# Final normalisation moved into the expert loop, one pair late, with fewer gathered-row buffers and interleaved rows

## The chip, the cores and the metric

One NeuronCore of a Trainium2 chip runs the whole program. The metric is the device time of one execution in microseconds, lower is better. Engine names are those of the profile: PE is TensorE, DVE is VectorE, ACT is ScalarE, POOL is GpSimd, SP is SyncE, which here only issues DMAs.

## What is computed

One step of a one-layer decoder for 512 prompt and 64 sample tokens of width D = 1024, all in float32. Two mixer branches (sliding-window attention and gated linear attention) and a first layer norm come before the part that is changed: a mixture of 32 experts, of which each token takes two of one group of eight, followed by the last layer norm.

```python
combine = jnp.sum(one_hot(e_glob, 32) * w[..., None], axis=1)   # two experts per token, of one group
for e in range(N_EXPERTS):
    he = jax.nn.silu(t @ w_g[e]) * (t @ w_u[e])                  # 1024 -> 256, twice
    y = y + combine[:, e:e + 1] * (he @ w_d[e])                  # 256 -> 1024
hp = layer_norm(DN_ALPHA * hp + y, ln2_g[l], ln2_b[l])           # (x - mean) * rsqrt(var + eps) * g + b
```

## The kernel before

The program runs straight through: mixer branches until about 640 us, then a router, then the **expert loop** from about 667 to 919 us, then a last stage. Only the router's tables, the loop and the last stage are touched.

**Pairs.** The experts are worked in pairs: pair g holds experts 2g and 2g+1, and a tile of 128 rows has 64 places for the tokens of each. With these inputs there are 16 pairs: pairs 0 to 14 are written out (`FIXED` = 15) and pair 15 is the one turn of a counted loop, which takes an expert with more than 64 tokens too. One pair's weights are six DMAs of 1 MB (gate, up and down of two experts), issued by SP into three slots (`NSLOT`); SP waits, before it loads pair g+3, until PE has used pair g (`gu_full`, `dn_full`).

**Rows.** The router builds tables: column g of `tbi` holds for each of the 128 places of pair g the token's row in `h1_rows` (the first layer norm's output) and the row of `expert_rows` to which the result goes; `tbw` holds the weight. An empty place has a row past the end, which the DMA's bounds check leaves out. `expert_rows` has 2 x 576 rows, one for each token and choice. POOL issues the row DMAs: `gather` (L698) brings rows into one of four buffers `Xg` (`NX` = 4), `send` (L707) takes the result tile `Yt` to `expert_rows`. The first four gathers go ahead of the loop; then pair by pair `send(g)`, `gather(g+4)`.

**One pair, engine by engine.** PE in turn g: `gate_up(g+1)` (L2030), `turn_a(g)` (L2038, a transpose of the activations), `turn_x(g+2)` (L2017, a transpose of gathered rows), `down(g)` (L2052). ACT: `silu(g+1)` (L1034), `drain_at(g)` (L1038, a copy out of PSUM that `down(g)` needs), `drain_xt(g+2)` (L1024, and L1027, which scales the gathered rows for the residual). DVE: `gate(g+1)` (L1590), `drain_xt(g+2)` (L1584), `scaled(g)` (L1598 and L1600), which adds weighted expert rows to the scaled rows, half a tile each, and releases POOL's `send(g)` and PE's `down(g+1)` (`y_rows`). Each engine runs its own queue in the order written here.

**Last stage.** When POOL has seen the last `send` land (`loop_done`), SP reads both results of each token back in five tiles (`y0`, `y1`); DVE adds them (L1626), subtracts the mean, and after ACT's squares and root (L1056 to L1062) scales (L1637); SP stores each tile.

Of the kernel before, what the change touches and what calls it, by code (L numbers as in the profile page):

```python
# [19 lines left out]
P = 128  # L20
D = 1024
# [5 lines left out]
TILES = 5  # L27
# [13 lines left out]
MAX_PAIRS = 25  # L41
# [3 lines left out]
NX, NY = 4, 1  # L45
# [11 lines left out]
for _n, _w in (("ident", 128), ("tri", 128), ("ones", 128), ("scan", T), ("bias", 2048), ("sbias", 272),  # L57
               ("cmask", 64), ("smask", 64), ("bmask", 8), ("i4", 4), ("i8", 8), ("i4v", 20), ("inval", 10), ("restart", 160), ("vals", 20), ("pid", 1), ("plow", 1), ("eid", 32), ("e31", 32), ("evens", 9),
               ("iota", 128)):
    CONST[_n] = (_at, _w)  # L60
    _at += _w
# [94 lines left out]
def layout():  # L156
# [59 lines left out]
def decoder_kernel(nc, A, O):  # L216
# [15 lines left out]
    with ctx:  # L232
# [80 lines left out]
        tbi = ctx.enter_context(nc.sbuf_tensor("tbi", [P, 2, COLS], i32))  # L313
        tbw = ctx.enter_context(nc.sbuf_tensor("tbw", [P, COLS], f32))
        w2 = ctx.enter_context(nc.sbuf_tensor("w2", [RANK, GH * HK], f32))
        y0, y1, junk2 = sb("y0", [P, TILES, D]), sb("y1", [P, TILES, D]), sb("junk2", [P, D])
        lst = ctx.enter_context(nc.sbuf_tensor("lst", [1, 132], i32))
        idx = ctx.enter_context(nc.sbuf_tensor("idx", [P, 2, 2], i32))
# [13 lines left out]
        for n, w in (("lg", 5 * 36), ("gmax", 5), ("gt", 20), ("gmin", 5), ("goh", 20), ("eg", 20), ("gsum", 5),  # L332
# [3 lines left out]
                     ("hot", 10 * COLS), ("eg1", 1), ("t9", 9), ("n9", 1)):  # L336
# [11 lines left out]
        y_d = nc.dram_tensor("expert_rows", [2 * TQ, D], f32, kind="Internal").ap()  # L348
# [4 lines left out]
        y_sum = sem("y_sum")  # L353
        y_sq = sem("y_sq")
# [36 lines left out]
        rows_moved = sem("rows_moved")  # L391
        max_ready = sem("max_ready")
# [114 lines left out]

        def wait_y_free(eng, g):
# [17 lines left out]
        def _(sp):  # L526
# [34 lines left out]
            def expert(g, a):  # L561
                return slice(2 * g + a, 2 * g + a + 1)
# [46 lines left out]

            sp.wait_ge(loop_done, 1)  # L610
            for i in range(TILES):
                r = ROWS[i]
                sp.dma_start(y0[0:r, i, :], y_d[i * P:i * P + r, :]).then_inc(y_back[i], 16)
                sp.dma_start(y1[0:r, i, :], y_d[TQ + i * P:TQ + i * P + r, :]).then_inc(y_back[i], 16)
            for i in range(TILES):
                sp.wait_ge(y_ready, i + 1)
                dst = O[0][0, i * P:i * P + P, :] if i < 4 else O[1].rearrange("b t d -> (b t) d")
                sp.dma_start(dst, y0[0:ROWS[i], i, :]).then_inc(y_out, 16)
            sp.wait_ge(y_out, 16 * TILES)

        @block.gpsimd
        def _(pool):
# [13 lines left out]
            for b in range(2):  # L636
# [3 lines left out]
                OUTS[0] += 1  # L640

# [45 lines left out]
            pool.wait_ge(h1_stored, 16 * TILES)  # L687
            pool.wait_ge(tb_ready, 1)
# [13 lines left out]
            def send(g, rows):  # L702
# [6 lines left out]
                                        bounds_check=2 * TQ - 1, oob_is_err=False).then_inc(y_sent[n], 16)  # L709
# [3 lines left out]
            for g in range(FIXED):  # L713
                send(g, tbi[:, 1, g:g + 1])
                if g + NX <= FIXED:
                    gather(g + NX, tbi[:, 0, g + NX:g + NX + 1])
            pairs = pool.value_load(lst[0:1, 128:129], min_val=FIXED + 1, max_val=MAX_PAIRS)
            with pool.Fori(FIXED, pairs) as g:
# [3 lines left out]
                hold(g)  # L722
                pool.tensor_copy(idx[:, :, :], tbi[:, :, bass.ds(g, 2)]).then_inc(idx_ready, 1)
# [4 lines left out]
                n, k = y_place(g)  # L728
                pool.wait_ge(y_sent[n], k * 16 + 16)
                hold(g)  # L730
            pool.sem_inc(loop_done, 1)
# [7 lines left out]
        def _(act):  # L739
# [299 lines left out]

            drain_xt(0)  # L1040
            silu(0)
            drain_xt(1)
            for g in range(FIXED):
# [3 lines left out]
                if g + 2 <= FIXED:  # L1047
                    drain_xt(g + 2)
            act.wait_ge(list_ready, 1)
            pairs = act.value_load(lst[0:1, 128:129], min_val=FIXED + 1, max_val=MAX_PAIRS)  # L1050
            with act.Fori(FIXED, pairs) as g:
                silu(g)
                drain_at(g)
                drain_xt(g + 1)

            link(act.activation(epsc[:, 1:2], epsc[:, 0:1], ACT.Sqrt))  # L1056
            for i in range(TILES):
                r = ROWS[i]
                act.wait_ge(y_sum, i + 1)
                link(act.activation(junk2[0:r, :], y0[0:r, i, :], ACT.Square, bias=mv[0:r, i, 0:1],  # L1060
                                    accum_out=mv[0:r, i, 1:2]))
                act.activation(rstd[0:r, i:i + 1], mv[0:r, i, 1:2], ACT.Sqrt, scale=1.0 / D, bias=epsc[0:r, 0:1])\  # L1062
                   .then_inc(y_sq, 1)


        @block.vector
        def _(dve):
# [343 lines left out]
            dve.tensor_copy(R["val"][:, 0:20], cst("vals"))  # L1411
# [107 lines left out]
            link(dve.scalar_tensor_tensor(R["nt"], R["nt"], 64.0, cst("e31"), ALU.mult, ALU.add))  # L1519
# [657 lines left out]
```

## Time and profile before

| | us |
|---|---|
| median of three runs (lowest to highest) | 955.76 (953.86 to 956.06) |
| the profiled execution | 955.62 |
| its span in the trace | 952.9 |
| PE busy | 826.7 (87%) |
| DVE busy | 407.4 (43%) |
| ACT busy | 274.8 (29%) |
| POOL busy | 73.8 (8%) |

The mean granted TensorE clock is 0.923 of full speed. The chain that ended last is PE for 68% of the span, DMA for 12%, DVE for 9%, SP's queue for 7%. These are averages over stages that differ: the mixers are PE's, while the expert loop moves over 100 MB of weights. What a change in the expert loop does is read from that loop's own rows: which wait ends last before each piece of PE's work.

### The profile page before, as it was taken

To read this page: it belongs to the slowest core of one execution; us is meant where nothing else is said; L and a number is where in the kernel's file an instruction comes from. 1 tells how busy PE (TensorE), PEld (TensorE's weight loads), DVE (VectorE), ACT (ScalarE), POOL (GpSimd) and SP (SyncE) were. 2 spreads that over 40 slices of the span, in tenths; PEclk is the share of its full clock that TensorE was granted. 3 is DMA by queue.
4 is the path that set the end of the run, shared out by engine and by line. 5 is a ranking of instruction groups with operands and counts; after the bars stand their busy time and mean duration, and the time that the engine had idled before them with its cause. 6 is when DMAs were issued, how large, how long until landed. Compare 5 with 4: busy or idle time off the path is not lost.

```text
span 952.9 us, 12647 instructions
## 1 busy us (share of the span) xinstructions
PE 826.7 (87%) x5254; PEld 636.2 (67%) x5254; DVE 407.4 (43%) x785; ACT 274.8 (29%) x530; POOL 73.8 (8%) x96
## 2 busy tenths in 40 slices
PE   2799999998999999999999989984999697786850
PEld 1789999885788878899999988774433232332320
DVE  4456644569625555732314166556122111111118
ACT  6367112335324345522122242120211011011113
POOL 1200300000000000000000010001011100101010
PEclk8899999999699999999999999995899998899875
DMA  9221533101114342222222064167999999999726
GB/s 322 95 90 60 188 122 94 45 13 33 45 50 125 109 133 72 86 70 89 67 89 79 33 251 161 41 239 315 397 417 418 421 417 418 421 419 420 303 94 238
DMA packets 65367, 178.70 MB, mean 188 GB/s; under 512 B 7168, under 2 KB 41184, under 8 KB 52880
## 3 DMA queue, kind: packets, MB, share of 16 engines
q1 hardware_dynamic: 53792, 144.45, 40.3%
q0 software_dynamic: 10832, 31.04, 9.3%
q10 hardware_dynamic: 688, 2.43, 0.7%
q8 instruction: 41, 0.67, 0.3%
q14 instruction: 14, 0.11, 0.0%
HBM read 165.33 MB, written 21.36 MB: 196 GB/s over the span
## 4 chain that ended last, share of the span: by engine, by line
PE 68%; DMA 12%; DVE 9%; SPq 7%; ACT 3%; issue 1%; ACTq 0%; POOLq 0%; DVEq 0%
PE bank L1658 16%; PE bank L1660 15%; PE bank L1659 15%; DMA wgu<-in_w_exp_up 10%; PE bank L2030 7%; SPq L554 6%; PE bank L2052 2%; PE bank L1866 1%; SPq L558 1%; PE bank L1766 1%; DVE ring L1121 1%; PE bank L1886 1%; PE bank L1895 1%; PE bank L1962 1%; PE bank L1879 1%
## 5 line engine op out<-in xcount | busy, mean ns | idle before, releaser
L1658 PE MATMUL bank<-hT,ring 128*128 128x288 f32 (+2 forms) x608 | 184.0, 303 | 15.5 <-DVE ring L1121 13.5
L1660 PE MATMUL bank<-hT,ring 128*128 128x288 f32 (+2 forms) x608 | 181.4, 298 | 0.0
L2030 PE MATMUL bank<-wgu,XT 128*64 128x512 f32 x512 | 131.0, 670 | 39.5 <-DMA wgu<-in_w_exp_up 37.8
L1658 PEld LDWEIGHTS bank<-hT,ring 128*128 128x128 f32 (+1 forms) x608 | 114.8, 189 | 21.8 <-DVE ring L1121 14.2
L2030 PEld LDWEIGHTS bank<-wgu,XT 128*64 128x64 f32 x512 | 44.4, 154 | 124.2 <-issue 117.6
L1660 PEld LDWEIGHTS bank<-hT,ring 128*128 128x128 f32 (+1 forms) x608 | 114.6, 189 | 0.6
L1121 DVE TENSOR_TENSOR ring<-ring,ring 128x2048 fp32r<-128x2048 f32 (+2 forms) x32 | 68.0, 2126 | 96.7 <-ACT ring L787 96.6
L787 ACT ACTIVATE ring<-ring 128x2048 fp32r<-128x2048 f32 (+2 forms) x32 | 56.1, 1752 | 112.9 <-PE bank L1660 112.2
L1590 DVE TENSOR_TENSOR act<-bank,sil 128x256 f32<-128x256 f32 x16 | 6.8, 424 | 159.4 <-PE bank L2038 143.3
L1659 PE MATMUL bank<-hlo_r,ring 128*128 128x288 f32 x240 | 70.7, 295 | 0.0
L1659 PE MATMUL bank<-osb,ring 128*128 128x288 f32 (+2 forms) x224 | 68.2, 304 | 0.0
L1034 ACT ACTIVATE sil<-bank 128x256 f32<-128x256 f32 x16 | 6.2, 385 | 195.8 <-PE bank L2030 195.8
L2052 PE MATMUL bank<-wd,aT 128*64 128x512 f32 x256 | 58.5, 598 | 1.2 <-ACT aT L1038 1.2
L1658 PE MATMUL bank<-ring,hT 128*128 128x256 f32 (+3 forms) x200 | 57.4, 288 | 0.4 <-ACT hlo_ln L938 0.4
L1659 PE MATMUL bank<-ring,hT 128*128 128x256 f32 (+3 forms) x200 | 56.0, 281 | 0.0
L1659 PEld LDWEIGHTS bank<-hlo_r,ring 128*128 128x128 f32 x240 | 45.2, 188 | 0.0
L1660 PE MATMUL bank<-ring,osb 128*128 128x256 f32 (+3 forms) x160 | 44.1, 277 | 0.0
L1659 PEld LDWEIGHTS bank<-osb,ring 128*128 128x128 f32 (+1 forms) x224 | 42.7, 190 | 0.6
L1659 PE MATMUL bank<-hlo_ln,ring 128*128 128x288 f32 x144 | 42.6, 296 | 0.0
L1658 PEld LDWEIGHTS bank<-ring,hT 128*128 128x128 f32 (+1 forms) x200 | 36.8, 184 | 4.9 <-issue 3.3
L1660 PE MATMUL bank<-gv,ring 128*128 128x288 f32 x128 | 37.7, 295 | 0.0
L1659 PE MATMUL bank<-gq,ring 128*128 128x288 f32 x128 | 37.7, 294 | 0.0
(351 smaller groups left out, 1485.6 us busy)
## 6 DMA issues: line engine op xcount, KB each, us to landing
wgu<-in_w_exp_gate SPq DMA_DIRECT2D x32, 1024.0 KB, 22.9
wgu<-in_w_exp_up SPq DMA_DIRECT2D x32, 1024.0 KB, 25.1
wd<-in_w_exp_down SPq DMA_DIRECT2D x32, 1024.0 KB, 27.0
ring<-in_w_in SPq DMA_DIRECT2D x17, 1024.0 KB, 5.2
ring<-in_w_in SPq DMA_DIRECT2D x8, 512.0 KB, 4.6
s<-in_state_gla POOLq DMA_DIRECT2D x4, 1024.0 KB, 6.1
out<-s POOLq DMA_DIRECT2D x4, 1024.0 KB, 5.1
ring<-in_w_gla_br SPq DMA_DIRECT2D x4, 1024.0 KB, 5.3
```

Of the source, the lines that this page charges most:

```text
L554: sp.dma_start(wgu[n][a][:, half], A[w][0][e, :, :].rearrange("e (p k) f -> p (e k) f", p=P))\
L558: sp.dma_start(wd[n][a][:, :, :], A["w_exp_down"][0][e, :, :].rearrange("e (p k) n -> p (e k) n", p=P))\
L787: act.activation(dst, src, ACT.Copy).then_inc(w_hi, 1)
L1121: dve.tensor_tensor(dst, src, high, ALU.subtract).then_inc(w_split, 1)
L1658: pe.matmul(out, sh, mh, start=first, stop=False)
L1659: pe.matmul(out, sh, ml, start=False, stop=False)
L1660: return pe.matmul(out, sl, mh, start=False, stop=last)
L1766: ins = pe.matmul(bk[:, c:c + 256], q, kT[rows, (a - 1) * P:(a + 1) * P], start=True, stop=True)
L1866: ins = pe.matmul(bk[:, 0:HV], kem[r:r + 64, b, c // 2, :], gv[r:r + 64, c // 2, gcol], start=True, stop=True)
L1879: pe.matmul(bk[:, 0:HV], am[:, b, i * P:i * P + P], gv[:, i, gcol], start=True, stop=False)
L2030: ins = pe.matmul(bk[t, :].rearrange("p (h f) -> p h f", h=2), XT[:, kc, t], wgu[n][a][:, :, kc, :], start=(kc == 0), stop=(kc == KC - 1))
L2052: ins = pe.matmul(psum[5 + half][t, :], aT[:, kc, t], wd[n][a][:, kc, 512 * half:512 * half + 512], start=(kc == 0), stop=(kc == 1))
```

## The change

1. **Last stage into the loop.** `expert_rows` becomes `first_rows` with one row per token. Experts are paired as g and g+16, so the two experts of a token (one group of eight) are never in one pair. The result of a token's first expert goes to `first_rows`; when its second expert's pair comes, those rows are fetched from there (`previous`) into one of two buffers `Pv`, added to that pair's `Yt`, normalised, and stored straight to the outputs. `tbi` gets two more columns for each pair: the rows to fetch (the same numbers serve the store to the prompt output), and the rows of the sample output.
2. **One pair late.** In turn g DVE runs `added(g-1)` ahead of `scaled(g)` and `normal(g-1)` behind it; ACT runs `squares(g-1)` behind `drain_xt(g+2)`, with a table load for the root and one back to Silu; POOL runs `finish(g-1)`, two stores, and `previous(g+1)`, behind `send(g)` and `gather(g+3)`. What is left of pair 14 stands between the written-out turns and the counted loop.
3. **Buffers.** `NX` goes from 4 to 3. `first_rows` is set once from the inputs, early, by two DMAs of POOL's queue, and both `Pv` buffers are zeroed.
4. **Interleaved rows.** Place k of an expert's 64 is no longer partition k of its half: eight neighbouring places stand four partitions apart.
5. **Tables.** `COLS` goes from 26 to 34; a pair past the sixteenth now holds 128 rows of one expert (none with these inputs).

```diff
-MAX_PAIRS = 25
+MAX_PAIRS = 33
 COLS = MAX_PAIRS + 1
-NX, NY = 4, 1
+NX, NY, NP = 3, 1, 2
@@ SP
             def expert(g, a):
-                return slice(2 * g + a, 2 * g + a + 1)
+                return slice(g + 16 * a, g + 16 * a + 1)
-            sp.wait_ge(loop_done, 1)
-            for i in range(TILES):
...
-            sp.wait_ge(y_out, 16 * TILES)
+            sp.wait_ge(rows_out, pairs * 32)
+            sp.sem_inc(all_stored, 1)
@@ POOL
+            pool.dma_start(y_d[0:SEQ, :], A["x_prompt"][0]).then_inc(y_set, 16)
+            pool.dma_start(y_d[SEQ:TQ, :], A["x_sample"].rearrange("b t d -> (b t) d")).then_inc(y_set, 16)
...
+            def previous(g, rows):
+                n, k = y_place(g - 1) if isinstance(g, int) else (FIXED % NY, g + (FIXED // NY - FIXED - 1))
+                pool.wait_ge(y_sent[n], k * 16 + 16)
+                hold(g)
+                n, k = prev_place(g)
+                pool.indirect_dma_start(out=Pv[n], out_offset=None, in_=y_d[:, :],
...
+            def finish(g, prompt, sample):
+                if not isinstance(g, int) or g:
+                    pool.wait_ge(z_ready, g)
+                    hold(g)
+                    rows = Ut
...
+                pool.indirect_dma_start(out=O[0][0], out_offset=bass.IndirectOffsetOnAxis(ap=prompt, axis=0), in_=rows,
+                                        in_offset=None, bounds_check=SEQ - 1, oob_is_err=False).then_inc(rows_out, 16)
+                pool.indirect_dma_start(out=O[1].rearrange("b t d -> (b t) d"),
...
                 if g + NX <= FIXED:
                     gather(g + NX, tbi[:, 0, g + NX:g + NX + 1])
+                if g == 0:
+                    pool.wait_ge(finish_ready, 1)
+                if g:
+                    finish(g - 1, tbi[:, 2, g - 1:g], tbi[:, 3, g - 1:g])
+                previous(g + 1, tbi[:, 2, g + 1:g + 2])
+            finish(FIXED - 1, tbi[:, 2, FIXED - 1:FIXED], tbi[:, 3, FIXED - 1:FIXED])
@@ ACT
+            def squares(g):
+                step(act.activation(epsc[:, 1:2], epsc[:, 0:1], ACT.Sqrt), g, 1)
+                act.wait_ge(z_sum, g)
+                for x in range(2):
+                    step(act.activation(last_bank[:, :], Pv[prev_place(g)[0]][:, 512 * x:512 * x + 512], ACT.Square, bias=z_stat[:, 0:1],
+                                        accum_out=z_stat[:, 1 + x:2 + x]), g, 2 + x)
...
+                step(act.activation(epsc[:, 1:2], epsc[:, 0:1], ACT.Silu), g, 5)
...
                 if g + 2 <= FIXED:
                     drain_xt(g + 2)
+                if g > 1:
+                    squares(g - 1)
+            squares(FIXED - 1)
@@ DVE
-                dve.tensor_tensor(rowhot[:, 5 * n:5 * n + 5, :], cst("iota").rearrange("p (c n) -> p c n", c=1)
+                dve.tensor_tensor(rowhot[:, 5 * n:5 * n + 5, :], cst("place").rearrange("p (c n) -> p c n", c=1)
...
+            def added(g):
+                pv = Pv[prev_place(g)[0]]
+                wait_previous(dve, g)
+                dve.wait_ge(y_rows, g + 1)
+                dve.scalar_tensor_tensor(pv, pv, 1.0, Yt[:, y_place(g)[0], :], ALU.mult, ALU.add, accum_out=z_stat[:, 3:4])\
+                   .then_inc(z_added, 1)
...
+            def normal(g):
+                dve.wait_ge(rows_out, g * 32)
+                dve.wait_ge(z_sum, g)
+                dve.scalar_tensor_tensor(Ut, Pv[prev_place(g)[0]], z_stat[:, 0:1], lng, ALU.add, ALU.mult).then_inc(u_done, 1)
...
+                dve.scalar_tensor_tensor(Ut, Ut, z_stat[:, 6:7], lnb, ALU.mult, ALU.add).then_inc(z_ready, 1)
...
                 if g + 2 <= FIXED:
                     drain_xt(g + 2)
+                if g > 1:
+                    added(g - 1)
                 scaled(g, tbw[:, g:g + 1])
+                if g > 1:
+                    normal(g - 1)
+            added(FIXED - 1)
+            normal(FIXED - 1)
```

What this does to two queues, at the places that the prediction speaks of. POOL before, the first gathers and turns 0 to 2 (`Xg` gathered rows, `Yt` the result tile):

```order
L698 DMA Xg_119<-h_rows,tbi 128x1024 x4
L707 DMA expert_rows<-Yt_121,tbi 1152x1024
L698 DMA Xg_119<-h_rows,tbi 128x1024
L707 DMA expert_rows<-Yt_121,tbi 1152x1024
L698 DMA Xg_119<-h_rows,tbi 128x1024
```

POOL after, the first gathers, turns 0 and 1, and turn 2 up to its stores (`Pv` fetched rows, `Ut` normalised rows; the stores from `lng` in turn 1 belong to pair 0, which has no token's second expert, so that all their rows are left out):

```order
L701 DMA Xg_119<-h_rows,tbi 128x1024 x3
L710 DMA first_rows<-Yt_121,tbi 576x1024
L701 DMA Xg_119<-h_rows,tbi 128x1024
L720 DMA Pv_80_128<-first_rows,tbi 128x1024
L710 DMA first_rows<-Yt_121,tbi 576x1024
L701 DMA Xg_119<-h_rows,tbi 128x1024
L733 DMA out<-lng_51,tbi 512x1024
L735 DMA out<-lng_51,tbi 64x1024
L720 DMA Pv_79_127<-first_rows,tbi 128x1024
L710 DMA first_rows<-Yt_121,tbi 576x1024
L701 DMA Xg_119<-h_rows,tbi 128x1024
L733 DMA out<-Ut_129,tbi 512x1024
```

Behind each `send` the gather now stands for the pair three ahead instead of four, and two stores and one fetch stand between it and the next `send`.

ACT before, the end of the written-out turns (turn 13, then `drain_at(14)`) and the beginning of the counted loop:

```order
L1034 ACTIVATE sil_122<-bank 128x256
L1038 ACTIVATE aT_124<-bank 128x256
L1024 ACTIVATE XT_120<-bank 128x512
L1027 ACTIVATE Xg_119<-Xg_119 128x1024
L1038 ACTIVATE aT_124<-bank 128x256
```

ACT after, the same turn 13 and `drain_at(14)`, L1074 being the old L1038 and `Pv_79` the rows of pair 12:

```order
L1070 ACTIVATE sil_122<-bank 128x256
L1074 ACTIVATE aT_124<-bank 128x256
L1060 ACTIVATE XT_120<-bank 128x512
L1063 ACTIVATE Xg_119<-Xg_119 128x1024
L1083 ACT_TABLE_LOAD
L1083 ACTIVATE small_54<-small_54 128x1
L1086 ACTIVATE bank,small_54<-Pv_79_127,small_54 128x512 x2
L1088 ACTIVATE small_54<-small_54 128x1
L1089 ACTIVATE small_54<-small_54 128x1
L1090 ACT_TABLE_LOAD
L1090 ACTIVATE small_54<-small_54 128x1
L1074 ACTIVATE aT_124<-bank 128x256
```

Seven instructions now stand between `drain_xt(15)` and the copy that `down(14)` needs. PE's order in the loop is as before.

## Rows read from the trace of the kernel before

**Rows 1.** Busy time by stretch: length; busy us (instructions) of PE, PEld, DVE, ACT, POOL; clock, DMA share, GB/s.
```profile
690.00:890.00 200.00, 165.70 (x740) 63.73 (x736) 32.91 (x50) 27.91 (x49) 25.36 (x25) 0.92 1.02 419
890.00:902.00 12.00, 9.09 (x46) 3.85 (x44) 2.62 (x4) 2.70 (x5) 0.99 (x1) 0.99 0.67 276
```

**Rows 2.** Timeline, one late pair: start us, busy us, engine, line, operation, count [idle before <-releaser].
```profile
844.41 1.01 POOL L707 DMA_INDIRECT expert_rows<-Yt,tbi  x1 [15.11 <-DVE Yt L1600]
846.53 8.78 PE L2030 MATMUL bank<-wgu,XT 128*64 128x512 f32 x32 [3.71 <-DMA wgu<-in_w_exp_up]
...
855.58 1.06 PE L2017 MATMUL bank<-const,Xg 128*128 128x128 f32 x8
856.57 3.65 PE L2052 MATMUL bank<-wd,aT 128*64 128x512 f32 x16
860.27 0.75 DVE L1600 SCALAR_TENSOR_TENSOR Yt<-bank,tbw,Xg 128x512 f32<-128x512 f32 x1 [0.87 <-PE bank L2052]
...
863.98 8.78 PE L2030 MATMUL bank<-wgu,XT 128*64 128x512 f32 x32 [3.76 <-DMA wgu<-in_w_exp_up]
```

**Rows 3.** Timeline, the first pairs.
```profile
692.01 7.04 PE L2030 MATMUL bank<-wgu,XT 128*64 128x512 f32 x32
692.23 0.75 DVE L1600 SCALAR_TENSOR_TENSOR Yt<-bank,tbw,Xg 128x512 f32<-128x512 f32 x1 [0.88 <-PE bank L2052]
693.81 1.02 POOL L707 DMA_INDIRECT expert_rows<-Yt,tbi  x1 [25.70 <-DVE Yt L1600]
695.14 1.03 POOL L698 DMA_INDIRECT Xg<-h_rows,tbi  x1 [0.31 <-issue]
...
699.32 1.06 PE L2017 MATMUL bank<-const,Xg 128*128 128x128 f32 x8
...
703.79 7.04 PE L2030 MATMUL bank<-wgu,XT 128*64 128x512 f32 x32
```

**Rows 4.** Waits of SP's own queue, 600 to 953 us: us in all, times, longest.
```profile
SPq L554 <- PE bank L2030: 32.3, 6, 8.6
```

**Rows 5.** Timeline, the last pairs and the last stage.
```profile
895.05 0.75 DVE L1600 SCALAR_TENSOR_TENSOR Yt<-bank,tbw,Xg 128x512 f32<-128x512 f32 x1 [0.87 <-PE bank L2052]
...
918.69 0.75 DVE L1600 SCALAR_TENSOR_TENSOR Yt<-bank,wsel,Xg 128x512 f32<-128x512 f32 x1 [0.90 <-PE bank L2052]
...
927.37 1.28 ACT L1056 ACT_TABLE_LOAD   x1
929.20 1.23 DVE L1626 SCALAR_TENSOR_TENSOR y<-y,y 128x1024 f32<-128x1024 f32 x1 [2.69 <-DMA y<-expert_rows]
930.71 1.15 ACT L1060 ACTIVATE junk<-y,small 128x1024 f32<-128x1024 f32 x1 [1.84 <-DVE small L1628]
...
931.99 0.29 ACT L1062 ACTIVATE small<-small 128x1 f32<-128x1 f32 x1
...
948.20 1.28 DVE L1637 SCALAR_TENSOR_TENSOR y<-y,small,lnb 64x1024 f32<-64x1024 f32 x1
```

**Rows 6.** DMA issues: queue, operation, count, median us from issue to landing; 690 to 697, then 640 to 953.
```profile
Xg<-h_rows,tbi POOLq DMA_INDIRECT x1, 10.3
...
Xg<-h_rows,idx POOLq DMA_INDIRECT x1, 2.2
expert_rows<-Yt,idx POOLq DMA_INDIRECT x1, 3.2
```

**Rows 7.** PE's timeline, three gate-ups after idle time.
```profile
742.83 7.09 PE L2030 MATMUL bank<-wgu,XT 128*64 128x512 f32 x32 [3.52 <-DMA wgu<-in_w_exp_up]
...
760.10 9.58 PE L2030 MATMUL bank<-wgu,XT 128*64 128x512 f32 x32 [5.28 <-DMA wgu<-in_w_exp_up]
...
776.96 7.09 PE L2030 MATMUL bank<-wgu,XT 128*64 128x512 f32 x32 [2.37 <-DMA wgu<-in_w_exp_up]
```

**Rows 8.** DVE's timeline, the router's table products.
```profile
655.79 0.77 DVE L1544 TENSOR_TENSOR onepair<-rs 128x260 f32<-128x260 f32 x2
```

**Rows 9.** The page's second part: mean busy share of the DMA engines, tenths, 40 slices.
```profile
DMA  9221533101114342222222064167999999999726
```

More of the change, by code:

```diff
@@ L347, in decoder_kernel @@
         h1_d = nc.dram_tensor("h1_rows", [TQ, D], f32, kind="Internal").ap()
-        y_d = nc.dram_tensor("expert_rows", [2 * TQ, D], f32, kind="Internal").ap()
+        y_d = nc.dram_tensor("first_rows", [TQ, D], f32, kind="Internal").ap()
         w2_in = sem("w2_in")
@@ L428, in decoder_kernel @@
         y_rows = sem("y_rows")
-        y_back = [sem(f"y_back{i}") for i in range(TILES)]
-        y_out = sem("y_out")
         out_done = sem("out_done")
-        y_ready = sem("y_ready")
-        loop_done = sem("loop_done")
+        finish_ready = sem("finish_ready")
+        prev_in = [sem(f"prev_in{n}") for n in range(NP)]
+        z_sum, z_step, z_sq, z_ready, u_done = sem("z_sum"), sem("z_step"), sem("z_sq"), sem("z_ready"), sem("u_done")
+        z_added, z_rstd, rows_out = sem("z_added"), sem("z_rstd"), sem("rows_out")
         OUTS = [0]
@@ L722, in _ @@
                 hold(g)
+                wait_previous(pool, g)
+                hold(g)
+                pool.wait_ge(rows_out, g * 32)
+                hold(g)
                 pool.tensor_copy(idx[:, :, :], tbi[:, :, bass.ds(g, 2)]).then_inc(idx_ready, 1)
@@ L727, in _ @@
                 gather(g + 1, idx[:, 0, 1:2])
[L728 to L731, printed above, removed]
+                finish(g, idx[:, 2, 0:1], idx[:, 3, 0:1])
+                previous(g + 1, idx[:, 2, 1:2])
             pool.wait_ge(out_done, 16 * OUTS[0])
@@ L1038, in drain_at, with step @@
                 act.activation(aT, psum[4][:, 0:F].rearrange("p (k c) -> p k c", k=2), ACT.Copy).then_inc(at_done, 1)
+            def step(ins, g, n):
+                ins.then_inc(z_step, 1)
+                act.wait_ge(z_step, 5 * g - 5 + n)
+            def squares(g):
[4 more added lines that the diff above has]
+                                        accum_out=z_stat[:, 1 + x:2 + x]), g, 2 + x)
+                step(act.activation(z_stat[:, 4:5], z_stat[:, 1:2], ACT.Identity, scale=1.0 / D, bias=epsc[:, 0:1]), g, 4)
+                act.activation(z_stat[:, 5:6], z_stat[:, 2:3], ACT.Sqrt, scale=1.0 / D, bias=z_stat[:, 4:5]).then_inc(z_sq, 1)
+                step(act.activation(epsc[:, 1:2], epsc[:, 0:1], ACT.Silu), g, 5)
             drain_xt(0)
@@ L1053, in _ @@
                 drain_at(g)
+                squares(g)
                 drain_xt(g + 1)
[L1056 to L1063, printed above, removed]
         @block.vector
@@ L1577, in _ @@
             dve.tensor_copy(tbw[:, :], last_bank[:, 0:COLS])
+            dve.wait_ge(h1_stored, 16 * TILES)
+            for n in range(NP):
+                dve.memset(Pv[n], 0.0)
             dve.tensor_copy(lst[0:1, 0:128], last_bank[0:1, P:2 * P]).then_inc(dve_drained, 1)
@@ L2121, in constants @@
     put("restart", np.tile(np.arange(5 * N_EXP) % 5 != 0, (P, 1)) * 1.0)
-    put("vals", np.concatenate([tok, tok, tok, tok + TQ], axis=1) - float(PAD_ROW))
-    put("iota", np.tile(np.arange(P), (P, 1)))
-    put("pid", p[:, None] - N_EXP)
-    put("plow", np.where(p < N_EXP, p, 0)[:, None])
-    put("evens", np.tile(2.0 * np.arange(9), (P, 1)))
-    put("eid", np.tile(64 * np.arange(N_EXP), (P, 1)))
-    put("e31", np.tile(64 * (31 - np.arange(N_EXP)), (P, 1)))
+    put("vals", np.concatenate([tok, tok], axis=1) - float(PAD_ROW))
+    put("iota", np.tile(np.arange(COLS), (P, 1)))
+    at = np.arange(64)
+    row = 32 * (at // 32) + 4 * (at % 8) + at // 8 % 4
+    place = np.zeros(P)
+    place[row], place[64 + row] = at, 64 + at
+    put("place", np.tile(place, (P, 1)))
+    put("pid", np.where(p < N_EXP, -1, (p - N_EXP) // 2)[:, None])
+    put("plow", np.where(p < N_EXP, p // 2 + 16 * (p % 2), 0)[:, None])
+    first = P * (np.arange(N_EXP) % 16) + 64 * (np.arange(N_EXP) // 16)
+    put("eid", np.tile(first, (P, 1)))
+    put("e31", np.tile(P * 16 - 64 - first, (P, 1)))
     return c
```

108 lines of the change are left out of this document (57 added, 51 removed).

## Prediction

> **What bounds the kernel now.** I read the busy shares by stretch first. From 690 to 890 us, the expert loop, the DMA engines are busy all the time and move 419 GB/s, while TensorE is busy 166 of 200 us [rows 1]. So the loop is paced by the expert weights, not by arithmetic. The timeline of one late pair says the same from TensorE's side: gate-up of one pair starts at 846.53, that of the next at 863.98, both after an idle of 3.7 us that the last w_up load ends. The period is 17.45 us [rows 2]. The first pairs run faster, because their weights were loaded ahead: gate-up starts at 692.01 and 703.79, a period of 11.78 us [rows 3]. SP waits for TensorE's gate-up 32.3 us in all, in six waits [rows 4]; the queue ahead stays full meanwhile [rows 1].
>
> After the loop comes a tail that nothing covers: the last expert rows are ready at 918.69 + 0.75 = 919.44, the span ends at 952.9, so 33.4 us go into sending, reading back, normalising five tiles and storing.
>
> I call y(g) the end of the second half of the `scaled` step of pair g. Before: y(0) = 692.23 + 0.75 = 692.98 [rows 3], y(13) = 895.05 + 0.75 = 895.80 and y(15) = 919.44 [rows 5]. The span is 895.80 + 23.64 + 33.4 = 952.9; the same three pieces are worked out for the changed kernel. The profiled execution took 955.62, so 2.7 us lie outside its span; the median of the runs, 955.76, is the same.
>
> **The tail: 10.6 instead of 33.4 us.** What is left behind y(15) is one pair: the sum (1.23), its mean (0.15, an estimate: half of ScalarE's small step of 0.29), the squares in two halves (1.15 by the full row, plus two read-outs and two small steps of up to 0.29, 2.2 in all), the reciprocal and one last pass of 1.28 [rows 5]; with the hops 5.4 us. POOL then issues two stores, the second 1.3 us after the first (the distance of its two issues in [rows 3]), 0.8 us after being released (692.98 to 693.81 [rows 3]), and a store without load behind it lands in 3.2 us [rows 6]. 5.4 + 0.8 + 1.3 + 3.2 = 10.7, taken as 10.6 since part of the first pass overlaps. Gain: 22.8 us. The Sqrt table load of 1.28 us [rows 5] lies ahead of the wait and costs nothing here.
>
> **The gather that lost its slack: the term that decides.** With four gathered-row buffers, gather(g+4) is issued behind send(g) and needed in iteration g+2. With three, gather(g+3) is issued at the same place and needed by `turn_x` in iteration g+1, where it stands before `down(g+1)` in TensorE's order. And y(g+1), after `down(g+1)`, releases the next send and gather. So there is now a ring through POOL's queue, once for each pair:
> y(g) to send issue 0.83, as above; send to gather issue 1.33 [rows 3]; the gather from issue to landing 10.3, while one that runs without the weights takes 2.2 [rows 6]; wake-up 0.1; turn_x to y, 855.58 to 861.02, 5.44 [rows 2]. Sum 18.0 us. TensorE then idles over 6 us before turn_x in the early pairs (turn_x stood at 699.32, the gather lands at 695.14 + 10.3 = 705.4 [rows 3]), and after an idle of 5.28 us the same gate-up took 9.58 instead of the 7.09 that it took after 2.37 us [rows 7]: 2.5 us more. 20.5 us for a pair that took 11.78.
> The send now carries half the valid rows, so the true latency may be some tenths shorter; the bounds of the ring are 18.0 (clock kept) and 20.5. I take 20.5 since the idle is nearer to 5.28 than to 2.37.
> How long does that last? Four pairs at 20.5 instead of 11.78 put TensorE 35 us behind, two periods of 17.45, which is what three weight slots can hold ahead. From there SP cannot issue, the queue runs empty at times, and a gather in such a gap lands in 2 to 3 us. The mean can then not be far from the weights' own 17.45. For the last two pairs no weights are behind them, and 11.8 holds. With a start later by 1.0 (below): y(13) = 694.0 + 4 x 20.5 + 7 x 17.45 + 2 x 11.8 = 921.8. Loss: 26.0 us.
>
> **From y(13) to y(15): 27 instead of 23.64 us.** The last pairs have no cover. On ScalarE the squares of pair 12 stand before the transposed-activation copy of pair 14. They cost two table loads of 1.28 and 2.2 of work, so that copy ends some 2.7 us after y(13); `down` 3.65 [rows 2] and the last half 0.8 give y(14) = +7.2. On VectorE normal(13), two passes of 1.28 and a reciprocal, ends at +10.7, the sum of pair 14 at +12.1. normal(14) rewrites `Ut` and must wait until finish(13) has landed: 10.7 + 0.4 + 1.3 + 3.2 = +15.6, then 2.9 to +18.5. Behind it on VectorE is queued gate(15), and TensorE waits for that: gate, turn_a, copy, down, last half, 6.3 with hops, is +24.8, and 2.5 for a clock that fell while TensorE waited. 27 us; without the clock 24.6. Loss: 3.4 us.
>
> **The rest.** Start: the row tables grow from 26 to 34 columns, so that the two table products, 0.77 together, and one like them grow by a third (0.4), and three small steps of about 0.2 are put before them [rows 8]; the first gather, and SP's third pair behind it, are later by 1.0 (0.5 to 2 with the two memsets).
> Inside the loop VectorE gets 4 us a pair (1.23, 0.15, twice 1.28, 0.15) and ScalarE 4.8; both are idle most of a 17.45 us period, so nothing, as long as they are not in front of the last pair as above.
> Rows moved: `first_rows` takes 576 rows instead of 1152, but 576 are fetched and 576 stored from the loop: 576 more rows of 4 KB, 2.36 MB, 5.6 us at 419 GB/s [rows 1]. In my sum they fall into the queue's gaps, 0; where the weights pace the loop, they cost 4 (the last pairs' come behind the weights).
> The two copies that preset `first_rows` (2.36 MB) go early on POOL's queue, where the DMA engines are busy two tenths [rows 9]: 0, at most 5.6.
>
> **Interleaved rows, and a page.** From 890 to 902 us the DMA share is 0.67 [rows 1]: the engines do not end together, and 0.33 x 12 = 4.0 us of their time is lost there. The Trainium skill, "DMA: Bandwidth & Descriptors", section "The descriptor swizzle", says that runs of four partitions go to one DMA engine and that each half of 64 partitions serves eight; by it rows packed from the start of a half load the first engines, and the interleaved places spread them. The trace agrees in that the ends are uneven. By that page the weights would end up to 4 us sooner, and the sum be the same, since the ring above sets it; only the first rival would go from 941 to 937.
>
> **Rivals.**
> (1) The gather is in time after all, and the loop keeps the weights' pace. For: in a late pair `turn_x` starts at 855.58, and a gather issued at 844.41 + 1.33 that takes 10.3 lands at 856.0, only 0.5 us late [rows 2, 6]. Against: the early pairs miss it by 6 us and nothing catches up. Then y(15) = 919.44 + 1 + 4 + 3.4 = 927.8, and 927.8 + 10.6 + 2.7 = 941.
> (2) The ring binds, but TensorE's clock stays: four pairs at 18.0 (-10.0) and an end without its 2.5: 962 - 12.5 = 950. For: after an idle of 3.52 us one gate-up took 7.09, no more than after 2.37. Against: 9.58 after 5.28, and the idles here are over 6 [rows 7].
> (3) POOL's queue becomes the pace. Under load one gather takes 8.1 us longer than alone behind one send [rows 6], about 4 us of queue for each of the two. Five DMAs a pair are then 20 us, over the period of 17.45, from which point it decides: 13 x 20.5 from 694 is y(13) = 960.5, and 960.5 + 27 + 10.6 + 2.7 = 1001. Against: as soon as the loop falls back, the weights leave gaps.
> The Trainium skill, "DMA: Bandwidth & Descriptors", section "Queues, rings and completion order", says that a DMA engine takes turns between queues packet by packet; the 10.3 against 2.2 agrees with that. It would make (3) likelier, not another time.
>
> **How the numbers follow.** Span 921.8 + 27 + 10.6 = 959.4, plus 2.7: 962 us, slower by 0.7%. Chances: forecast 0.60 (955 to 972), (1) 0.17, (2) 0.15, (3) 0.06, something else 0.02. A measurement tells 0.3% from no change here, 2.9 us: 952.9 to 958.6 is "same". Of the forecast 0.06 lies there, of (2) 0.07 (it reaches from 946 to 955). Faster 0.17 + 0.08 = 0.25, same 0.13, slower 0.54 + 0.06 + 0.02 = 0.62. The range goes from 944, into (1), to 974.
>
> **What would show it.** TensorE's wait before turn_x on the gather in pairs 3 to 6, 5 us or more, and y(4) near 694 + 4 x 20.5 = 776 instead of 692.98 + 4 x 11.78 = 740: the ring. y(1) near 706 would show the ring wrong from the start. SP waiting for gate-up far longer than 32 us, and a DMA share under 1.0 between 760 and 890. y(13) to y(15) near 27. The last pair's tail near 10.6; if it is over 15, a store or the table load was missed.

## The result, and the profile after

The changed kernel takes 984.08 us (median of four runs, 982.13 to 985.62) beside 954.81 us of the kernel before: a ratio of 1.0314, 95% interval 1.0296 to 1.0332, so 3.1% slower. The prediction was 962 us, with a range of 944 to 974. The sign and the ring of the first pairs were right; how long the ring holds, and what ends the span, were not. The profiled execution has a span of 982.2 us. Where its time stands, in the pieces of the prediction (y(g) is the end of the second half of `scaled` of pair g, L1600 before and L1657 after):

| piece | before | forecast | after | off by |
|---|---|---|---|---|
| start of the program to y(0) | 693.0 | 694.0 | 696.5 | +2.5 |
| y(0) to y(13) | 202.8 | 227.8 | 240.9 | +13.1 |
| y(13) to y(15) | 23.6 | 27.0 | 26.6 | -0.4 |
| y(15) to the end of the span | 33.4 | 10.6 | 18.2 | +7.6 |
| span | 952.9 | 959.4 | 982.2 | +22.8 |

TensorE's timeline of the changed kernel, turns 1 and 4 (start us, busy us, then what it did and what ended the idle time before it; L2084 is `turn_x`, L2119 `down`, L2097 gate-up):

```profile
708.99 1.97 PE L2084 MATMUL bank<-const,Xg 128*128 128x128 f32 x8 [5.94 <-DMA Xg<-h_rows,tbi]
710.89 5.76 PE L2119 MATMUL bank<-wd,aT 128*64 128x512 f32 x16
716.49 7.03 PE L2097 MATMUL bank<-wgu,XT 128*64 128x512 f32 x32
...
767.33 1.16 PE L2084 MATMUL bank<-const,Xg 128*128 128x128 f32 x8 [2.18 <-DMA Xg<-h_rows,tbi]
768.42 3.65 PE L2119 MATMUL bank<-wd,aT 128*64 128x512 f32 x16
```

This answers to [rows 3]: `turn_x` of the early pairs now stands 5.94 us idle for the gather, and after that idle `turn_x` takes 1.97 instead of 1.06 us and `down` 5.76 instead of 3.65 us; after 2.18 us of idle they take 1.16 and 3.65. The granted clock of the two stretches (columns as in [rows 1]) is 0.60 and 1.00:

```profile
708.00:717.00 9.00, 8.01 (x28) 3.46 (x30) 1.74 (x3) 1.54 (x2) 0.00 (x0) 0.60 1.02 418
767.00:773.00 6.00, 5.67 (x30) 2.60 (x32) 3.57 (x7) 4.38 (x7) 1.04 (x1) 1.00 1.01 417
```

So the ring costs its waits and a slower clock behind the long ones: behind the nine waits of 4.4 us and more, `turn_x` and `down` together take 1.7 to 3.0 us longer than the 4.71 us of before. The waits of TensorE over the whole loop, and those of SP's queue from 690 us on (us in all, times, longest):

```profile
PE bank L2084 <- DMA Xg<-h_rows,tbi: 61.8, 14, 7.1
```

```profile
SPq L567 <- PE bank L2119: 136.6, 13, 17.3
SPq L563 <- PE bank L2097: 67.7, 11, 7.2
```

The same two waits of SP's queue in the kernel before, also from 690 us on ([rows 4] counts from 600):

```profile
SPq L554 <- PE bank L2030: 16.5, 4, 6.0
SPq L558 <- PE bank L2052: 10.2, 5, 3.2
```

Where TensorE waited for weights before [rows 2], it now waits for gathered rows, 14 times, and SP, which waited 16.5 us for gate-ups and 10.2 for `down`, waits 67.7 and 136.6. TensorE's waits for weights are gone. By stretch, the answer to the two rows of [rows 1]:

```profile
690.00:890.00 200.00, 152.06 (x640) 58.10 (x638) 63.28 (x98) 72.03 (x134) 54.90 (x52) 0.86 0.99 392
890.00:902.00 12.00, 7.57 (x32) 3.24 (x30) 3.16 (x6) 5.19 (x9) 1.88 (x2) 0.86 0.29 109
```

The granted clock fell from 0.92 to 0.86 and the bytes from 419 to 392 GB/s; between 890 and 902 us the weights, which before came to their end here, pause (no load is on its way from 895.3 to 902.1) and go on until 930.8. The DMA issues of 690 to 900 us say how long a gather takes in this loop:

```profile
Xg<-h_rows,tbi POOLq DMA_INDIRECT x11, 9.9
```

The end, which answers to [rows 5] (L1657 `scaled`, L1679 the last pass of `normal`, L733 and L735 the stores of pair 15, L720 a fetch for a pair that does not follow):

```profile
963.22 0.75 DVE L1657 SCALAR_TENSOR_TENSOR Yt<-bank,wsel,Xg 128x512 f32<-128x512 f32 x1 [0.90 <-PE bank L2119]
...
968.15 1.28 DVE L1679 SCALAR_TENSOR_TENSOR Ut<-Ut,small,lnb 128x1024 f32<-128x1024 f32 x1
...
970.32 1.00 POOL L733 DMA_INDIRECT out<-Ut,idx  x1 [2.48 <-DVE Ut L1679]
...
971.63 0.98 POOL L735 DMA_INDIRECT out<-Ut,idx  x1 [0.31 <-issue]
...
972.91 1.05 POOL L720 DMA_INDIRECT Pv<-first_rows,idx  x1 [0.30 <-issue]
```

The second store lands at 973.86, 9.9 us after y(15), as forecast (10.6). But the span ends at 982.2. What stands there is in no busy row; the records of the engines' own queues have it:

```
after:  POOL DRAIN (end of the block) 971.75 to 981.96; last row DMA's issue ends 973.96
before: POOL DRAIN (end of the block) 924.13 to 929.19; last row DMA's issue ends 922.66
```

Every engine's queue closes with a drain. GpSimd's ends 8.0 us behind the issue of its last row DMA here. In the kernel before it began 1.5 us behind that issue, took 5.05 us, lay under the last stage and cost nothing.

### The profile page after: what moved, and what is told of

Read it like the earlier page. It is cut to its first block, busy times and chain, and to the rows that moved or that the text cites. A ratio compares the mean times of both kernels' runs of the same rounds, so it can differ in the third digit from the quotient of the medians.

```text
span 982.2 us, 13003 instructions
## 1 busy us (share of the span) xinstructions
PE 841.1 (86%) x5254; PEld 641.1 (65%) x5254; DVE 448.4 (46%) x853; ACT 343.2 (35%) x663; POOL 128.8 (13%) x146
## 4 chain that ended last, share of the span: by engine, by line
PE 67%; DMA 15%; DVE 8%; ACT 4%; issue 3%; POOL 2%; POOLq 0%; ACTq 0%; DVEq 0%; SPq 0%
PE bank L1725 15%; PE bank L1726 14%; PE bank L1727 14%; DMA Xg<-h_rows,tbi 12%; PE bank L2119 7%; PE bank L2084 3%; PE bank L2097 2%; POOL first_rows L710 2%; PE bank L1933 1%; DVE Yt L1657 1%; DMA ring<-in_w_out 1%; PE bank L1833 1%; DVE ring L1167 1%; PE bank L1953 1%; PE bank L1962 1%
## 5 line engine op out<-in xcount | busy, mean ns | idle before, releaser
L2097 PE MATMUL bank<-wgu,XT 128*64 128x512 f32 x512 | 115.5, 604 | 1.9 <-ACT XT L1060 1.9
L2097 PEld LDWEIGHTS bank<-wgu,XT 128*64 128x64 f32 x512 | 37.5, 140 | 76.4 <-issue 73.9
L2084 PE MATMUL bank<-const,Xg 128*128 128x128 f32 x136 | 28.3, 375 | 67.6 <-DMA Xg<-h_rows,tbi 61.8
L2119 PE MATMUL bank<-wd,aT 128*64 128x512 f32 x256 | 77.4, 759 | 4.1 <-ACT aT L1074 4.1
L2084 PEld LDWEIGHTS bank<-const,Xg 128*128 128x128 f32 x136 | 22.9, 211 | 72.2 <-DMA Xg<-h_rows,tbi 63.8
L2119 PEld LDWEIGHTS bank<-wd,aT 128*64 128x64 f32 x256 | 21.5, 175 | 49.8 <-issue 45.6
L1641 DVE COPY XT<-bank 128x512 f32<-128x512 f32 x17 | 11.8, 691 | 79.4 <-PE bank L2084 79.2
L1060 ACT ACTIVATE XT<-bank 128x512 f32<-128x512 f32 x17 | 10.1, 597 | 102.1 <-PE bank L2084 102.1
```

The lines of the kernel that those rows point to most:

```text
L1060: act.activation(XT[:, 0:4, :], psum[0][:, :].rearrange("p (k c) -> p k c", k=4), ACT.Copy)\
L1641: dve.tensor_copy(XT[:, 4:8, :], psum[1][:, :].rearrange("p (k c) -> p k c", k=4)).then_inc(xt_dve, 1)
L2084: ins = pe.transpose(psum[k // 4][:, k % 4 * P:k % 4 * P + P], Xg[:, m, k:D:KC], ident)
L2097: ins = pe.matmul(bk[t, :].rearrange("p (h f) -> p h f", h=2), XT[:, kc, t], wgu[n][a][:, :, kc, :], start=(kc == 0), stop=(kc == KC - 1))
L2119: ins = pe.matmul(psum[5 + half][t, :], aT[:, kc, t], wd[n][a][:, kc, 512 * half:512 * half + 512], start=(kc == 0), stop=(kc == 1))
```

## The experiments

Theory R: with three gathered-row buffers the ring from y(g) over send and gather to `turn_x` and y(g+1) sets the loop's pace. Rival W: the five row DMAs of a pair set it, by their turns in POOL's queue (the prediction's third rival). What was left open by the trace of after: why the ring held for all 13 pairs, and what the end waits for.

| kernel | y(0) | y(13) | y(15) | span | median us | ratio to before, 95% |
|---|---|---|---|---|---|---|
| before | 693.0 | 895.8 | 919.4 | 952.9 | 953.8 to 954.8 | |
| changed | 696.5 | 937.4 | 964.0 | 982.2 | 984.08 | 1.0296 to 1.0332 |
| before, three buffers | 693.3 | 936.1 | 953.3 | 987.0 | 988.28 | 1.0326 to 1.0394 |
| changed, four buffers | 695.6 | 901.5 | 933.8 | 952.1 | 952.71 | 0.9973 to 1.0004 |
| changed, gather first | 696.5 | 908.8 | 936.2 | 954.5 | 956.42 | 1.0014 to 1.0045 |
| changed, `turn_x` late | 695.0 | 901.0 | 932.1 | 950.3 | 954.43 | 0.9985 to 1.0031 |
| before, interleaved rows | 694.6 | 893.2 | 915.2 | 948.1 | 949.94 | 0.9930 to 0.9966 |
| changed, four and two out | 694.2 | 897.3 | 927.2 | 945.4 | 949.94 | 0.9944 to 0.9973 |
| changed, no down loads | 696.1 | 885.8 | 912.0 | 930.2 | (one run, 932.21) | |

### One part alone: the kernel before with three buffers

```diff
-NX, NY = 4, 1
+NX, NY = 3, 1
```

> The kernel before with one edit: three gathered-row buffers instead of four; nothing of the normalisation moves. Theory R (the ring y(g) to send to gather(g+3) to turn_x(g+3) to y(g+1) through three buffers sets the loop): from y(0) = 693 to y(13) the changed kernel took 240.8 us, the kernel before 202.8; with the same ring here y(13) is near 934 and the whole near 955 + 38 = 993 (985 to 998), with TensorE waiting 5 us or more before turn_x on the gather in most pairs. Theory W (the five row DMAs of a pair, their turns in POOL's queue, set the pace of the changed kernel): this kernel has only two row DMAs per pair, so at most the clock and a few early pairs are lost, 955 to 965.

988.28 us. Its waits of TensorE and its gathers (median us to landing):

```profile
PE bank L2017 <- DMA Xg<-h_rows,tbi: 62.1, 13, 7.0
```

```profile
Xg<-h_rows,tbi POOLq DMA_INDIRECT x11, 9.6
```

The waits are those of the changed kernel (62.1 and 61.8 us), with two row DMAs a pair instead of five. Theory R holds and W is out: one buffer less costs 34 us by itself, more than the 29.3 that the whole change loses.

### One part undone: four buffers in the changed kernel

```diff
-NX, NY, NP = 3, 1, 2
+NX, NY, NP = 4, 1, 2
-    inside("h1", [("Xg", NX * D), ("Yt", NY * D), ("Pv1", D)])
+    inside("h1", [("Xg", NX * D), ("Yt", NY * D)])
+    at["Pv1"] = at["onepair"]
```

The second fetched-row buffer takes the place of a router table that is free by then.

> The changed kernel with four gathered-row buffers again (one fetched-row buffer put elsewhere), everything else as changed. Theory R: no gather is late, the loop goes back to the weights' pace, y(13) is 895.8 + 3.6 (later start) + 0 to 4 (more rows) = 899 to 903 instead of 937.4, and the whole is 984 - 36 = 948 (944 to 952). Theory W: the five row DMAs are as many as before, so the period stays near 18.5 and the time at 975 or more.

```profile
PE bank L2099 <- DMA wgu<-in_w_exp_up: 34.1, 9, 5.7
PE bank L2107 <- DVE act L1649: 8.3, 1, 8.3
...
PE bank L2086 <- DMA Xg<-h_rows,tbi: 0.5, 1, 0.5
```

The wait for gathers falls from 61.8 to 0.5 us and that for weights is back; y(13) is 901.5, inside the forecast's 899 to 903. The whole, 952.71, lies just above the forecast's upper end of 952: y(13) to y(15) grew to 32.3 us, of which 8.3 are the wait for the last gate in the second line.

### The ring made shorter: gather ahead of send

```diff
-                send(g, tbi[:, 1, g:g + 1])
                 if g + NX <= FIXED:
+                    pool.wait_ge(y_rows, g + 1)
                     gather(g + NX, tbi[:, 0, g + NX:g + NX + 1])
+                send(g, tbi[:, 1, g:g + 1])
```

> The changed kernel, three buffers, but POOL issues gather(g+3) ahead of send(g) instead of behind it; both wait for the same y(g). Theory R: the ring loses the 1.33 us of the send's issue and what the gather waited for the send's rows in the queue, so it takes 14.4 to 16.7 us, under the weights' 17.45; y(13) falls to 901 to 908 and the whole to 948 to 955. If only the 1.33 us go (the gather still takes 10.3), the early pairs still idle TensorE and it is 960 to 968. Theory W: the same DMAs in another order, no change, 981 to 987.

```profile
PE bank L2085 <- DMA Xg<-h_rows,tbi: 39.1, 14, 4.4
```

```profile
Xg<-h_rows,tbi POOLq DMA_INDIRECT x13, 8.4
```

956.42 us. Two DMAs in another order give back 27.7 of the 29.3 us lost. The gather, with the send no longer ahead of it, lands in 8.4 instead of 9.9 us, and the longest wait is 4.4 instead of 7.1. The mean period is (908.8 - 696.5) / 13 = 16.3 us; the 956.42 lies just above the forecast's 948 to 955.

### The ring cut: turn_x behind down

```diff
                 turn_a(g)
-                if g + 2 <= FIXED:
-                    turn_x(g + 2)
                 down(g)
+                if g + 2 <= FIXED:
+                    turn_x(g + 2)
```

VectorE's copy of its result moves behind `scaled(g)` likewise.

> The changed kernel, three buffers, gather behind send, but TensorE runs turn_x(g+2) behind down(g) instead of ahead of it, and VectorE copies its result out behind scaled(g). Theory R: a late gather no longer delays y(g); it has to land only before gate_up(g+2), so the ring spans two pairs, 12.4 + 1.1 + 0.8 + 7 + 0.6 + 0.5 + 3.6 + 0.9 = 27 us for two, 13.5 for one, under 17.45; the loop goes to the weights' pace, y(13) near 903, the whole near 950 (946 to 956; about 1 us per pair is lost where gate_up waits for the copy, hidden while weights set the pace). Theory W: no change, 981 to 987.

```profile
717.71 3.65 PE L2119 MATMUL bank<-wd,aT 128*64 128x512 f32 x16 [0.47 <-ACT aT L1074]
721.29 1.16 PE L2084 MATMUL bank<-const,Xg 128*128 128x128 f32 x8
723.28 7.09 PE L2097 MATMUL bank<-wgu,XT 128*64 128x512 f32 x32 [0.83 <-ACT XT L1060]
```

954.43 us with y(13) at 901.0: three buffers and the gather behind the send, but y(g) no longer waits for a gather. In these rows `turn_x` follows `down` without a wait, gate-up starts 0.83 us behind it, and the early pairs take 13.6 us for the 13.5 of the forecast.

### Why a gather takes 10 us: the down loads left out

```diff
                 sp.wait_ge(dn_full[n], k)
-                for a in range(2):
-                    down_in(experts[a], n, a)
```

> The changed kernel with three buffers as changed, but the down weights are loaded for the first three pairs alone and used again by the later ones (so a part of the experts' result is that of other weights); 4.2 instead of 6.3 MB are loaded for a pair, and nothing is loaded in answer to down(g), just ahead of the gather. Theory Q (a gather takes 10 us because its rows take turns with the weights that SP was released to load right before it): the gate and up loads of a pair are through in 10 us, a gather issued after that lands in 2.2 to 4 us, the ring is 10 to 12 us, TensorE's own 11.8 to 13 a pair set the loop, and y(13) is 850 to 866 instead of 937. Rival P (the 10 us are POOL's own: the send ahead of it and the stores and fetches): gathers keep 8 us or more, the period stays above 15, y(13) is 895 or more.

```profile
PE bank L2081 <- DMA Xg<-h_rows,tbi: 24.5, 9, 6.0
```

```profile
Xg<-h_rows,tbi POOLq DMA_INDIRECT x13, 6.2
```

y(13) falls to 885.8, the wait for gathers to 24.5 us. In turns 1 to 8 the gathers take 3.8 to 4.1 us and 6.2 to 6.7 us by turns, the longer ones where two or more gate and up loads are still on their way, and the periods alternate between 11.8 to 12.0 and 14.7 to 16.2. Later one gather takes 9.65 us, with two gate and up loads issued 0.6 and 0.2 us ahead of it and two more just behind. That is theory Q's direction, and P's 895 is not reached, but neither is Q's 850 to 866: it took the gate and up loads to be through in time, and in every second pair they were not. Fewer loads at the gather's own moment and fewer loads in all go together in this run, so that by itself it does not tell the two apart.

The trace of the changed kernel does. Ahead of each of the 13 gathers issued from 698 to 926 us, SP issues two down loads, 2.5 to 3.1 us before. The four that found those two alone on their way, with nothing else issued in the next 3.6 us, took 5.9 to 7.0 us. The eight that found gate or up loads left over as well took 8.5 to 10.2 us, and one with four gate and up loads issued within 1.7 us behind it took 11.2. So a gather is slow because of the loads around it, and those just ahead of it are there in every pair:

```profile
812.83 0.80 SPq L567 DMA_DIRECT2D wd<-in_w_exp_down  x2
...
814.37 1.28 POOL L710 DMA_INDIRECT first_rows<-Yt,tbi  x1 [10.42 <-DVE Yt L1657]
815.95 1.13 POOL L701 DMA_INDIRECT Xg<-h_rows,tbi  x1 [0.31 <-issue]
```

`down(g)` ends, SP issues two more down loads, y(g) follows, then send and gather: the same event fills the queue and releases the gather into it. This pair is one of the four where nothing else was left over; its gather took 6.05 us. The DMA share of two single microseconds around it (last column but one) shows the queue nearly empty just before the down loads, and full when the gather enters:

```profile
812.00:813.00 1.00, 1.00 (x6) 0.28 (x4) 0.16 (x1) 0.94 (x4) 0.00 (x0) 1.00 0.32 135
815.00:816.00 1.00, 1.00 (x6) 0.28 (x4) 1.00 (x1) 0.00 (x0) 0.69 (x2) 1.00 0.99 418
```

### Interleaved rows alone, in the kernel before

```diff
-                dve.tensor_tensor(rowhot[:, 5 * n:5 * n + 5, :], cst("iota").rearrange("p (c n) -> p c n", c=1)
+                dve.tensor_tensor(rowhot[:, 5 * n:5 * n + 5, :], cst("place").rearrange("p (c n) -> p c n", c=1)
```

> The kernel before with one edit: the interleaved places of the rows; the same rows move, to other partitions. If uneven ends of the DMA engines cost what the rows of before suggest (a share of 0.67 over the last 12 us of the weights), the weights end up to 4.0 us sooner and the time is 950 to 953. If the row DMAs' places do not matter because each transfer's end is set by turns in a full queue, it stays within 0.3% of before, 951 to 956.

949.94 us, 0.5% faster. The two stretches of [rows 1]:

```profile
690.00:890.00 200.00, 169.02 (x762) 65.95 (x762) 34.71 (x53) 31.12 (x54) 25.36 (x25) 0.93 1.02 419
890.00:902.00 12.00, 8.53 (x36) 2.92 (x34) 1.61 (x3) 0.80 (x2) 0.99 (x1) 0.91 0.87 360
```

In the last 12 us the DMA share rises from 0.67 to 0.87, and y(0) to y(13) takes 198.6 instead of 202.8 us: 4.2 us, for 4.0 read from the share. The last weight tile lands 210.6 instead of 215.6 us after y(0). The prediction's sentence from the Trainium skill, "DMA: Bandwidth & Descriptors", section "The descriptor swizzle", agrees with this in direction; the share is a mean of all engines, so that no run here shows which engine serves which partitions, or how evenly single engines end.

### What ends the span

> The changed kernel without what its last turn prepares for a pair after it (gather(16), previous(16), turn_x(16) and its copies), which these inputs do not have. Theory D (the span ends when GpSimd's closing drain does, 8.0 us after the end of its last row DMA's issue, 973.96 to 981.96 in the changed kernel): only the fetch behind the two stores goes, so the drain ends 1.3 us sooner after y(15), tail 16.9 instead of 18.2. Rival (the drain's length follows the number of row DMAs still on the way): two of five go and the drain is shorter than 6.5 us behind the last store's issue, tail below 15.5.

> The kernel before with one row DMA more: after the last stage's last tile is ready, GpSimd issues one gather whose rows are all left out (they are past the end). Theory D: the closing drain follows it and ends 6.5 to 8.0 us after the end of its issue, near 949.5 + 0.9 + 1.0 + 6.5 to 8.0 = 958 to 959.5, so the span grows by 5 to 6.6 us and its tail from 33.4 to 38.5 to 40. Rival (in the changed kernel the end waits for the landing of data, not for the drain): a DMA without data lands in about 2 us, the span grows by 1 us at most.

Each of these two kernels was run once. Their POOL rows at the end, first of the changed kernel without the next pair's preparation, then of the kernel before with a late gather:

```profile
969.95 0.98 POOL L733 DMA_INDIRECT out<-Ut,idx  x1 [4.15 <-DVE Ut L1676]
971.23 0.96 POOL L735 DMA_INDIRECT out<-Ut,idx  x1 [0.30 <-issue]
```

```profile
949.00 1.02 POOL L698 DMA_INDIRECT Xg<-h_rows,tbi  x1 [28.25 <-DVE y L1639]
```

```
no next pair: POOL DRAIN ends 980.03, 7.8 behind the end of the last issue (972.19); span 980.3, tail 16.6
late gather:  POOL DRAIN ends 955.16, 5.1 behind the end of the last issue (950.02); span 955.4, tail 37.9
```

In the second kernel SP's last tile landed at 951.17 and the empty gather at 951.40; the span went on for 4.0 us until the drain was over. So the closing drain ends the span, not a landing: theory D. The first run's tail is 16.6 for D's 16.9, and its rival's 15.5 is not reached. The second run's is 37.9: above the rival's 34.4 at most, but below D's 38.5 to 40, for the drain's length is no constant, as D had it. Counted from the drain's start or the end of the last issue, whichever is later, it is 5.05 us in the kernel before, 5.1 with the late gather, 7.8 behind two stores and 8.0 behind two stores and a fetch. What it depends on was not separated.

### A version with the repairs

Four buffers, and a second buffer for the normalised rows with a semaphore of its own, so that `normal(g)` waits for the stores of pair g-2 (`out_place(g)` is g % 2 and g // 2):

```diff
-                dve.wait_ge(rows_out, g * 32)
+                n, k = out_place(g)
+                Ut = Uts[n]
+                dve.wait_ge(rows_out[n], k * 32)
```

> The changed kernel with four gathered-row buffers (as in the run with four) and two buffers for the normalised rows in turn, so that normal(g) waits for the stores of pair g-2, not g-1. In the run with four, normal(13) waited 3.0 us and normal(14) 3.2 us for those stores, and TensorE stood 8.3 us behind the last gate. Theory E (the last pairs lose time to that wait): y(14) to y(15) falls from 22.2 to about 18, the whole from 952.7 to 948 to 949.5. Rival (the squares in ScalarE's queue or the send of pair 13 hold the end): no change, 951 to 954.

```profile
PE bank L2120 <- DVE act L1660: 6.0, 1, 6.0
PE bank L2099 <- DMA Xg<-h_rows,idx: 5.8, 1, 5.8
PE bank L2134 <- ACT aT L1086: 4.1, 2, 3.4
```

949.94 us, faster than both kernels (0.9944 to 0.9973 of before), and between theory E's 948 to 949.5 and its rival's 951 to 954. The wait for the last gate falls from 8.3 to 6.0 us and y(14) to y(15) from 22.2 to 19.7, 2.5 of the 4.2 us that theory E wanted: with the stores out of the way the sum of pair 14 waits 2.58 us for its fetched rows. It is no faster than the kernel before with interleaved rows alone. Against that kernel the moved normalisation gains 14.7 us in the tail (32.9 to 18.2) and loses 4.4 in y(0) to y(13) (198.6 to 203.0) and 7.9 in y(13) to y(15) (22.0 to 29.9).

## Why the prediction was wrong, by its own steps

**What bounds the kernel before, and the ring: right.** For the 20.5 us of the forecast the changed kernel's first three periods were 20.9, 20.5 and 20.7, with the gather at 10.2, 9.9 and 10.0 us against 10.3 taken. Putting the clock's 2.5 us in was right too: 3.0, 3.0 and 2.8 measured, though in `turn_x` and `down` and not in the gate-up from which the size was taken. Rival (2) falls, and rival (3) with the kernel before on three buffers (its price took 20.5 us a pair, where its own five turns of 4 us make 20).

**How long the ring lasts: the step that failed, 13.1 of the 22.8 us.** The prediction let a gather land in 2 to 3 us in a gap of the queue, held the mean near the weights' 17.45 from the fifth period on, and gave the last two pairs 11.8 each, "no weights" being behind them. The mean of the 13 periods is 240.9 / 13 = 18.5; ten of the 13 are between 16.6 and 20.9, and the three short ones (14.2, 14.0, 13.8) follow gathers of 5.9 to 6.3, none of 2 to 3. By the prediction's own terms, the first four took 76.3 us for 82.0, the next seven 130.0 for 122.2, and the last two 34.6 for 23.6. The gaps exist (0.32 at 812 us), but not where the gather is: SP's loads are released by `down(g)` just ahead of y(g), so the queue is full again when the gather enters it. The forecast took the two as independent; both hang on the same event. In the last two pairs the weights were not through, because a loop that holds TensorE back also holds back SP's releases (its waits above): gate and up loads went out at 905.4 to 906.9, the gather issued at 905.2, just ahead of them, took 11.2 us, and the last down load landed at 930.8.

Nor were 2 to 3 us to be had in a gap. The 2.2 us of [rows 6] are those of a gather for a pair that does not follow, and it moves no rows. The packets of the same gather in the changed kernel, 966 to 968 us:

```profile
DMA packets 144, 0.00 MB, mean 0 GB/s; under 512 B 144, under 2 KB 144, under 8 KB 144
```

Gathers with rows that met no load took 3.4 us (at 663.1 in the kernel before), 3.9 (at 664.9 in the changed one) and 3.7 (at 876.4 without down loads). So the loads add 6.4 to 6.9 us to a gather of 10.3, not the 8.1 of rival (3).

**The tail: 18.2 instead of 10.6.** The terms up to the second store's issue held within 0.1 us each, and its landing took 2.2 instead of 3.2 (9.9 us in all against 10.6). What was missing is a term that the kernel before hides: GpSimd's closing drain, which ends 8.0 us behind its last row DMA. The forecast took the last landing for the end of the span; in the kernel before, where SP stores last, SP's last landing at 952.4 is followed by the span's end at 952.9. The sign given for a tail over 15, a missed store or table load, pointed to the wrong place.

**The start: +3.5 instead of +1.0.** 1.1 us of it was there ahead of the router's table products (656.88 against 655.79), where profiles differ by more (654.33 to 657.49 in those of the kernel before and its three variants). From the table products to y(0) it is 39.7 instead of 37.2: 0.7 us up to the first gather, where 1.0 was taken, and 1.8 from there to y(0), where the first gate-up took 9.90 instead of 8.85. The bound of 2 was a little low.

**y(13) to y(15): right**, 26.6 for 27, and by the waits named: `normal(14)` 3.23 us for the stores of pair 13, TensorE 4.4 for the last gate, 4.1 in two waits for the activation copies behind the squares. y(14) came at +9.2 instead of +7.2, since `down(14)` took 5.3 instead of 3.65; that did not reach the end, as normal(14), which started at +16.3 for the +15.6 forecast, set it.

**Rows moved, 0 in the sum:** no run shows this term by itself in a loop bound by the ring. With four buffers y(0) to y(13) takes 4.4 to 7.3 us more than in the interleaved kernel before (203.0 and 205.9 for 198.6), near rival (1)'s 4; what else the normalisation does to the loop is in that too. **Rival (1)** itself is the kernel with four buffers: 952.7, not 941, by the drain (7.6) and a longer end.

## What to carry to other kernels

When buffers are cut, write down who releases the next fill and what else the same event releases: a prefetch whose slack goes can be slowed by what is issued at its own moment, whatever the mean load of the queue. Before time is called saved in a last stage, look at what else ends there under cover, the engines' closing drains among it. A change in several parts should be measured in parts: here the interleaved rows gain 0.5%, the moved normalisation is about even once its buffers are whole, and one gathered-row buffer less (4 KB of each partition) loses 3.6%.

## What the runs showed of the hardware

Rows that the bounds check leaves out still make packets. The page's count of packets of before and after:

```profile
DMA packets 65367, 178.70 MB, mean 188 GB/s; under 512 B 7168, under 2 KB 41184, under 8 KB 52880
```

```profile
DMA packets 70396, 176.41 MB, mean 180 GB/s; under 512 B 13297, under 2 KB 47313, under 8 KB 57857
```

The bytes hardly change, but the packets under 512 B grow by 6129. The changed kernel issues 48 row DMAs more (16 fetches, 32 stores), 6144 places, most of them left out. The late gather behind the last stage, whose 128 rows are all left out, shows such packets alone: POOL's queue from 949.2 to 952 us (packets, MB, share of 16 engines):

```profile
q0 software_dynamic: 144, 0.00, 2.3%
```

2.3% of 16 engines for 2.8 us is some 7 ns a packet, so that 6129 of them are an estimated 2.7 us of all 16 engines over the whole program: small beside the 34 us that one buffer less costs. What they cost a gather in its queue was not measured by itself. And GpSimd's drain at the end of the program, which ends 5.1 to 8.0 us behind its last row DMA's issue, is a price that a kernel which ends on that queue pays in full.
